# Rounded two-pass products, paired inner products and moved copies in a two-block transformer kernel

## The reference

```python
gdn_qkv = jax.nn.silu(causal_dwconv(gdn_qkv, gdn_conv_w))
g_q = l2_normalize(g_q) * (GDN_HEAD_DIM ** -0.5); g_k = l2_normalize(g_k)
t_inv = lax.linalg.triangular_solve(eye + m, eye, left_side=True, lower=True)   # 64x64 per chunk and head
def step(state, xs):
    v_new = u_c - w_c @ state
    o = q_c @ state + qk_c @ v_new          # qk_c @ v_new: the inner product
    state = state * gl + k_c.T @ v_new
```

```python
q_b = _rotary(q_d, DIFF_ROT); k_b = _rotary(k_d, DIFF_ROT)      # 16 of 64 channels turned
merged = sigmoid(...) * (y_a @ w_branch_a) + sigmoid(...) * (y_b @ w_branch_b)
x = _layer_norm(DEEPNORM_ALPHA * x + merged @ w_out, ...)
```

## Time and profile before

| | |
|---|---|
| median of 3 runs | 1514.75 us (1513.74 to 1515.01) |
| profiled execution | 1514.83 us, span 1513.0 us |
| TensorE products busy | 1496.9 us (99%), 11622 records |
| VectorE, ScalarE, GpSimd busy | 947.8, 811.1, 250.5 us |
| DMA | 266.26 MB, mean 176 GB/s |
| chain that ended last | TensorE 94%, VectorE 4%, ScalarE 1% |

### The profile page before, as it was taken

One profiled execution on the slowest core, in us unless ns is written; L12 is line 12 of the kernel. 1 busy time (PEld: TensorE's weight loads), 2 busy tenths in 40 slices (PEclk: granted clock), 3 DMA queues, 4 the chain that ended last, 5 costly groups with the idle time before them and its releaser, 6 DMA issues.

```text
span 1513.0 us, 27372 instructions
## 1 busy us (share of the span) xinstructions
PE 1496.9 (99%) x11622; PEld 1384.2 (91%) x11622; DVE 947.8 (63%) x1379; ACT 811.1 (54%) x1249; POOL 250.5 (17%) x140
## 2 busy tenths in 40 slices
PE   9999999999999999999999999999999999999998
PEld 8998898889998889998898989998789999899997
DVE  6655466776555475654558685655477766767756
ACT  6554376545544364554574554544365675555762
POOL 0000252113000260000432040000430004500041
PEclk9999999999999999999999999999999999999999
DMA  9655464236555456555543155555455344553341
GB/s 384 226 195 194 159 210 143 79 110 229 190 196 195 167 204 222 195 195 190 195 173 113 59 190 200 194 195 195 167 209 195 112 140 152 208 188 136 131 149 56
DMA packets 39720, 266.26 MB, mean 176 GB/s; under 512 B 4460, under 2 KB 4716, under 8 KB 9392
## 3 DMA queue, kind: packets, MB, share of 16 engines
q1 hardware_dynamic: 38304, 260.13, 48.8%
q0 software_dynamic: 720, 3.35, 0.6%
q10 hardware_dynamic: 576, 1.05, 0.2%
HBM read 263.46 MB, written 1.05 MB: 175 GB/s over the span
## 4 chain that ended last, share of the span: by engine, by line
PE 94%; DVE 4%; ACT 1%; DMA 0%; issue 0%; SPq 0%; DVEq 0%
PE PS L487 17%; PE PS L488 17%; PE PS L489 16%; PE PS L501 6%; PE PS L503 6%; PE PS L502 6%; PE PS L559 4%; PE PS L562 4%; PE PS L560 4%; PE PS L470 1%; PE PS L471 1%; PE PS L472 1%; PE PS L614 1%; PE PS L1942 1%; DVE rawL L319 1%; PE PS L1351 1%
## 5 line engine op out<-in xcount | busy, mean ns | idle before, releaser
L487 PE MATMUL PS<-xTH,WH 128*128 128x256 f32 x2256 | 641.2, 284 | 0.0
L488 PE MATMUL PS<-xTL,WH 128*128 128x256 f32 x2256 | 628.7, 279 | 0.0
L489 PE MATMUL PS<-xTH,rawL 128*128 128x256 f32 x2256 | 626.6, 278 | 0.0
L316 ACT ACTIVATE WH<-raw 128x1024 fp32r<-128x1024 f32 (+2 forms) x476 | 484.6, 1048 | 131.1 <-PE PS L562 101.3
L319 DVE TENSOR_TENSOR rawL<-raw,WH 128x1024 fp32r<-128x1024 f32 (+1 forms) x395 | 481.4, 1245 | 102.5 <-ACT WH L316 102.2
L487 PEld LDWEIGHTS PS<-xTH,WH 128*128 128x128 f32 x2256 | 423.6, 188 | 9.2 <-issue 6.7
L488 PEld LDWEIGHTS PS<-xTL,WH 128*128 128x128 f32 x2256 | 423.7, 188 | 3.4 <-issue 2.9
L489 PEld LDWEIGHTS PS<-xTH,rawL 128*128 128x128 f32 x2256 | 424.9, 188 | 0.0
L319 POOL TENSOR_TENSOR rawL<-raw,WH 128x1024 fp32r<-128x1024 f32 (+1 forms) x81 | 196.1, 2443 | 1049.8 <-ACT WH L316 1049.8
L316 ACT ACTIVATE sg<-PS 128x256 f32<-128x256 f32 x79 | 30.3, 384 | 177.6 <-PE PS L489 177.6
L319 DVE TENSOR_TENSOR hh<-PS,sg 128x256 f32<-128x256 f32 x79 | 33.5, 424 | 144.7 <-ACT sg L316 144.7
(11 more groups left out here) (366 smaller groups left out, 2004.7 us busy)
## 6 DMA issues: line engine op xcount, KB each, us to landing
raw<-in_weights SPq DMA_DIRECT2D x233, 1024.0 KB, 4.8
gb<-in_lngb SPq DMA_DIRECT2D x16, 512.0 KB, 5.1
raw<-in_weights SPq DMA_DIRECT2D x2, 1056.0 KB, 4.9
gb<-in_ln SPq DMA_DIRECT2D x4, 512.0 KB, 4.5
cst<-in_consts POOLq DMA_DIRECT2D x1, 1378.5 KB, 10.4
x0T<-in_xT ACTq DMA_DIRECT2D x4, 256.0 KB, 5.5
raw<-in_weights SPq DMA_DIRECT2D x4, 256.0 KB, 5.1
xt<-in_x POOLq DMA_DIRECT2D x1, 1024.0 KB, 17.3
```

The source lines that it names most:

```text
L316: return Q.put("act", waits, lambda e: e.activation(out, in_, func, **kw))
L487: e.matmul(out, c, xTH[:, k, :], start=k == 0, stop=False)
L488: e.matmul(out, c, xTL[:, k, :], start=False, stop=False)
L489: ins = e.matmul(out, u.L(i, 128 * k, 128), xTH[:, k, :], start=False, stop=k == KD - 1)
```

## The change

- `squares`: ScalarE squares into `sqH` (rounded), VectorE forms `sqL = sq - sqH`, and TensorE makes two rounded passes with a rounded matrix of ones. The same for `rotary` with `permR`: copy, low part `rl`, two passes; the cosine product now reads PSUM.
- The copy of T goes from VectorE to ScalarE.
- The inner products of chunks 0 and 1, and of 2 and 3, go together, in turn on two quadrants.
- In the tail of the second block no split goes to GpSimd.

```diff
@@ mix
+                                h = act(sqH[m][:, :].rearrange("p (j s) -> p j s", j=2), dst, ACT.Square, [a, sq_free[m]])
+                                conv_ready[nm, i] = (m, y, h)
...
         def squares(nm, i):
-            m, a = conv_ready[nm, i]
+            m, y, h = conv_ready[nm, i]
             b, free = bank("B")
-            p = pe([a, free], lambda e: e.matmul(PS[:, b, :], ones, sq[m][:, :], start=True, stop=True))
+            lo = tt(sqL[m][:, :], sq[m][:, :], sqH[m][:, :].bitcast(F32), ALU.subtract, [y, h])
+            def fn(e):
+                e.matmul(PS[:, b, :], onesR[:, :], sqH[m][:, :], start=True, stop=False)
+                return e.matmul(PS[:, b, :], onesR[:, :], sqL[m][:, :], start=False, stop=True)
+            p = pe([ones_rounded(), h, lo, free], fn)
...
-            T_ready = copy(T[:, :, :], PS[:, b, :].rearrange("p (i s) -> p i s", i=8), [p])
+            T_ready = act(T[:, :, :], PS[:, b, :].rearrange("p (i s) -> p i s", i=8), ACT.Copy, [p])
...
+        def inner(c):
+            bs = {x: bank("B") for x in (c - 1, c)}
+            def fn(e):
+                for h in range(4):
+                    for x, (b, _) in bs.items():
+                        R = slice(64 * (x % 2), 64 * (x % 2) + 64)
+                        ins = e.matmul(PS[other(x), b, 128 * h:128 * h + 128], Eu[R, 4 * (x // 2) + h, :], news[x][0][:, h, :], start=True, stop=True)
+                return ins
+            p = pe([news[c - 1][1], news[c][1], qt[c // 2], [free for _, free in bs.values()]], fn)
...
+            if a_ == 1:
+                inner(c)
+                out_sum(c - 1)
+                out_sum(c)
...
@@ second, rotary
             a = act(w[:, :, :], v2(b), ACT.Copy, [p, rw_free[i]])
-            release(b, a)
-            c = tt(pr[:, :, :], w[:, :, :], two(C("dcos")), ALU.mult, [a, pr_free[0]])
+            lo = tt(wl[:, :, :], v2(b), w[:, :, :].bitcast(F32), ALU.subtract, [a])
+            c = tt(pr[:, :, :], v2(b), two(C("dcos")), ALU.mult, [p, pr_free[0]])
+            release(b, a, lo, c)
...
-                p2 = pe([a, free], lambda e: e.matmul(PS[:, b2, :], C("perm"), w[:, :, :].rearrange("p j s -> p (j s)"), start=True, stop=True))
+                    e.matmul(PS[:, b2, :], permR[:, :], w[:, :, :].rearrange("p j s -> p (j s)"), start=True, stop=False)
+                    return e.matmul(PS[:, b2, :], permR[:, :], wl[:, :, :].rearrange("p j s -> p (j s)"), start=False, stop=True)
+                p2 = pe([perm_ready, a, lo, free], fn)
...
@@ second, tail
-        st["share"] = True
+        pump(st["split"] + 1)
```

More of the change, by code:

```diff
@@ L852, in ffn, with ones_rounded @@
         yield
+    ones_ready = []
+    def ones_rounded():
+        if not ones_ready:
+            ones_ready.append(act(onesR[:, :], ones, ACT.Copy, [par_ready]))
+        return ones_ready[0]
     PLE_AT = 55 * 1024
@@ L975, in mix @@
         sq = [put_at("sqa", [128, 512], 12), put_at("sqb", [128, 512], 14)]
+        sqH = [put_at("sqHa", [128, 512], 63, F32R), put_at("sqHb", [128, 512], 65, F32R)]
+        sqL = [put_at("sqLa", [128, 512], 12, F32R), put_at("sqLb", [128, 512], 14, F32R)]
         rs = [put_at("rsa", [128, 512], 16), put_at("rsb", [128, 512], 61)]
@@ L1582, in gate @@
             gate_ready[t] = split(gH[:, :, T_], gL[:, :, T_], yg[t][:, :, :], [y])
+        def inner(c):
[7 more added lines that the diff above has]
+            p = pe([news[c - 1][1], news[c][1], qt[c // 2], [free for _, free in bs.values()]], fn)
+            for x, (b, _) in bs.items():
+                outs_[x] = (b, p, qss[x])
+        news, qss = {0: (u_[0:64, 0, :, :], uts[0])}, {0: None}
         for c in range(4):
@@ L1586, in mix @@
             R, Ro = slice(64 * a_, 64 * a_ + 64), other(c)
-            qs = None
             if c == 0:
-                new, newt = u_[R, 0, :, :], uts[0]
                 next(fill)()
@@ L1598, in mix @@
                 p = pe([state, wts[c], qts[c], free], fn)
[L1599 to L1604, removed]
+                newt = tt(vn[R, :, :], u_[R, t, :, :], PS[R, b, :].rearrange("p (h s) -> p h s", h=4), ALU.subtract, [p, uts[t]])
+                news[c] = vn[R, :, :], newt
+                if c == 2:
+                    normed(0)
+                qss[c] = act(os_[Ro, :, :], PS[Ro, b, :].rearrange("p (h s) -> p h s", h=4), ACT.Copy, [p, on_ready.get(c - 2), qts_all])
+                release(b, newt, qss[c])
                 if c < 3:
@@ L1607, in mix @@
                              ALU.mult, [state, glt], "pool")
-                out_sum(c - 1)
                 next(fill)()
@@ L1611, in mix @@
                 b, free = bank("B")
+                new, newt = news[c]
                 def fn(e, b=b, t=t, R=R, new=new):
@@ L1625, in mix @@
                 sb_soft(0)
[L1626 to L1637, removed]
+            if c == 2:
+                normed(1)
+            if a_ == 1:
+                inner(c)
+                out_sum(c - 1)
+                out_sum(c)
+                if c == 1:
+                    rms(0)
+                    rms(1)
+                else:
+                    gate(0)
             next(fill)()
+        rms(2)
+        go(1)
+        rms(3)
         normed(2)
-        out_sum(3)
-        go(2)
-        rms(3)
         go(2)
         normed(3)
-        go(1)
+        go(2)
         pump(len(chunks))
@@ L1675, in second @@
         va = put_at("va", [128, 2, 512], 32)
-        rw = [put_at("rwa", [128, 2, S], 36), put_at("rwb", [128, 2, S], 38)]
+        rw = [put_at("rwa", [128, 2, S], 36, F32R), put_at("rwb", [128, 2, S], 38, F32R)]
+        rl = [put_at("rla", [128, 2, S], 70, F32R), put_at("rlb", [128, 2, S], 72, F32R)]
+        rs_, permR = put_at("rsum", [128, 2, S], 74), put_at("permR", [128, 128], 76, F32R)
         pr = put_at("pr", [128, 2, S], 40)
@@ L1742, in second @@
         xw = [xT_ready[0], xT_ready[1], par_ready]
+        perm_ready = act(permR[:, :], C("perm"), ACT.Copy, [xw])
         lp = PAR(l, "lam", 0, 256).rearrange("p (a b d) -> p a b d", a=2, b=2)
@@ L1785, in rotary, with fn @@
             rw_n[0] += 1
-            w = rw[i]
+            w, wl = rw[i], rl[i]
             a = act(w[:, :, :], v2(b), ACT.Copy, [p, rw_free[i]])
-            release(b, a)
-            c = tt(pr[:, :, :], w[:, :, :], two(C("dcos")), ALU.mult, [a, pr_free[0]])
+            lo = tt(wl[:, :, :], v2(b), w[:, :, :].bitcast(F32), ALU.subtract, [a])
+            c = tt(pr[:, :, :], v2(b), two(C("dcos")), ALU.mult, [p, pr_free[0]])
+            release(b, a, lo, c)
             def later():
                 b2, free = bank("B")
-                p2 = pe([a, free], lambda e: e.matmul(PS[:, b2, :], C("perm"), w[:, :, :].rearrange("p j s -> p (j s)"), start=True, stop=True))
-                s = tt(w[:, :, :], v2(b2), two(C("dsin")), ALU.mult, [p2, c])
+                def fn(e):
+                    e.matmul(PS[:, b2, :], permR[:, :], w[:, :, :].rearrange("p j s -> p (j s)"), start=True, stop=False)
+                    return e.matmul(PS[:, b2, :], permR[:, :], wl[:, :, :].rearrange("p j s -> p (j s)"), start=False, stop=True)
+                p2 = pe([perm_ready, a, lo, free], fn)
+                s = tt(rs_[:, :, :], v2(b2), two(C("dsin")), ALU.mult, [p2, c])
                 release(b2, s)
-                y = tt(dst, pr[:, :, :], w[:, :, :], ALU.add, [s, c])
+                y = tt(dst, pr[:, :, :], rs_[:, :, :], ALU.add, [s, c])
                 rw_free[i] = y
```

8 lines of the change are left out of this document (3 added, 5 removed).

## The result

The changed kernel takes 1538.61 us (median of 4 runs, 1538.1 to 1540.6) against 1514.88 us of the kernel before beside it: ratio 1.016, 95% interval 1.0143 to 1.0178, 23.7 us slower. Its profiled execution spans 1536.6 us (before: 1513.0).

A forecast was written before the change was run, and what follows sets the result against it. TensorE, busy 1496.9 of 1513.0 us, was taken to bound the kernel. Gains of 15.9 against costs of 31.4, mostly 28.0 of `squares` waits, gave net +15.5: 1514.8 to 1530.3 us; own range 1525 to 1537, 8-in-10 range 1520 to 1545.

The forecast's parts named there:

- likeliest case: The forecast itself: whole kernel net +15.5 us, to 1530.3 us; chance 0.62.
- rival 1: TensorE's clock falls in the new `squares` waits, slowing products behind them: up to 16 us, half taken, 1538; chance 0.22.
- passes on TensorE, `squares` and rotary: 16 constant-matrix products in two rounded passes instead of one fp32 product: gain 0.40 us each, 6.4 in all.
- k0, k1, q0 waits: At `squares`, TensorE waits for `sqL` behind VectorE's six convolution steps: 2.3, 4.3 and 4.3 us a layer.
- q1 waits: At `squares` of q1, `sqL` stands behind three normalisations and a weight split: wait 3.1 us a layer.
- Gram products: Their 0.5 us of waiting goes, since q1's wait lets VectorE catch up.
- inner products: Pairs of chunks alternating on two quadrants cost what one chunk did: gain 4.0 us, bounds 0 to 4.0.
- `scL` and tail of the chunks: Moved VectorE sums and one more split ahead of the short convolution's low part: +0.3 us, at most 2 x 1.22.
- rotary, whole edit: Second block: 3.2 us gained on passes, against waits of 0.7 at the permutation and 2.4 for a bank.
- tail splits: Second block: twice seven splits move from GpSimd to VectorE; the `mt` wait goes, -0.7 us, bounds -0.7 and +1.4.
- The round trip: At `squares` of k1 and q0, TensorE to ScalarE to VectorE and back: an unshortened wait of 4.3 us each.
- third rival: At `squares`, `sqL` is there when TensorE comes, in all eight places: the 28.0 us go, 1502.3; chance 0.06.

The follow-up runs named there:

- wait_filled: Changed kernel with small fp32 products queued on TensorE ahead of the `squares` products of k0, k1, q0 and q1; 1533.8 us, ratio 1.013.
- sq_undone: Changed kernel with the `squares` products back in one fp32 product, all else as changed; 1508.58 us, ratio 0.9963.
- t_alone: Kernel before with only the copy of T moved to ScalarE; 1510.78 us, ratio 0.9971.
- rot_sq_undone: Changed kernel with both `squares` and rotary products back in fp32; 1508.55 us, ratio 0.9958.
- share_back: Changed kernel with all rounded products back in fp32 and every second tail split on GpSimd again; 1509.49 us, ratio 0.9967.
- sq_alone: Kernel before with the `squares` edit alone; 1547.43 us, ratio 1.0214.
- lo_early: Changed kernel with the `sqL` subtraction queued right behind the squares, ahead of the next pair's six convolution steps on VectorE; 1523.63 us, ratio 1.0063.
- split_held: Changed kernel with all rounded products in fp32 and no weight split queued during the last two quarters ahead of the mix's output product; 1505.97 us, ratio 0.9945.
- early_no_share: As `lo_early`, but weight splits stay on VectorE while k and q are projected; 1512.33 us, ratio 0.9981.
- lo_pool: Changed kernel with `sqL` of k0, k1, q0 on GpSimd, no shared splits there, k1's product a quarter later, q1 in fp32; 1512.41 us, ratio 0.9982.
- after: The changed kernel itself, with all edits, against the kernel before; 1538.61 us, ratio 1.016.

## Why the prediction was right, and where it was off

The sign, the place and the mechanism of the waits were right: slower, at `squares`, behind the convolution steps. The time of the likeliest case (1530.3) was 8.3 us short of the measured; the range held because rival 1, the falling clock, is what happened. The failed step is that choice: the forecast took the 4.3 us waits as too short for the clock to fall, at 0.62 against 0.22. Its own sign of being wrong, the granted clock leaving full speed after the waits, came true; that the range still holds the time is due to its having been widened for rival 1.

| term | predicted, us | shown |
|---|---|---|
| passes on TensorE, `squares` and rotary | -6.4 | not measured alone; a rounded pass is 0.23, the first behind a wait 0.31 |
| k0, k1, q0 waits | +21.8 | 21.2 in the list, 22.1 from start to start |
| q1 waits | +6.2 | 0: the slow stretch filled them (in `wait_filled` 2.9 and 2.8 are back) |
| Gram products | -0.5 | -0.5: gone from the list, though q1 did not wait |
| low clock | 0 (rival 1: +8) | about 10.2, of which 4.8 on the path (`wait_filled`) |
| `squares`, whole edit | +24.8 | +29.5 to +30.0 (`sq_undone`) |
| T | -4.3 | -4.3 (`t_alone`) |
| inner products | -4.0 | 3.9 by the distance of the traces |
| `scL` and tail of the chunks | +0.3 | `scL` +1.7, `ez` +1.3 |
| rotary, whole edit | -0.1 | 0 within some 0.8 (`rot_sq_undone`) |
| tail splits | -0.7 | -0.8 in waits (`share_back`); 13 splits left GpSimd (77 to 64), not 14 |

- **The round trip.** The estimate of 4.3 us a wait, made from TensorE's arrival, ScalarE's scaled copies, the six steps and the subtraction, came out at 4.15 and 4.16. VectorE sat idle for 4.92 us before those steps, and the subtraction's inputs were there from 225.70 on, 4 us before the steps began: only the order in the queue held it.
- **The clock.** Five of six such waits were followed by the low level. After 4.2 us it came every time, here and in `sq_alone` (eight of eight). After 1.8 to 2.3 us it came in seven of ten cases: one of two here, two of two in `sq_alone`, four of six in `lo_early`. After waits of up to 1.4 us it never came. So the argument that a 4.3 us wait is too short between stretches of dense work failed clearly: in most cases half of that was enough. Rival 1 gave +8 by halving a bound of 16, and found the hidden part in q1. Its sum (1538) met the measured time partly by luck: on the path the clock cost 5 us in place of 8, and the other 3 us or so came from the chunks.
- **The chunks.** The inner products gained what two quadrants promised:

```profile
311.07 0.32 PE L1607 MATMUL PS<-u,Eu 64*64 64x128 f32 x1
311.08 0.32 PE L1607 MATMUL PS<-vn,Eu 64*64 64x128 f32 x1
...
312.09 0.38 PE L487 MATMUL PS<-xTH,WH 128*128 128x256 f32 x1
```

  Eight products in 1.02 us, two starting 0.01 apart, where four took 1.01. But the term of +0.3, bounded by 2 x 1.22, took a value near the wrong end of its bounds: it was 1.7 at `scL`. Its reason was wrong too: not one split more stands ahead of `scL`, but one sum (`split_held`). The wait of 0.3 for `ez` a layer was not named at all; its distance grows by 0.6 there, 1.3 in both. What moved ahead of `ez` on VectorE was not tried apart.
- **Rotary.** The waits are those predicted, 0.6 and 0.3 at the permutation (0.7 predicted) and 1.3 and 1.0 at the value product (2.4). The list puts the 1.3 down to `kT`, whose last piece ahead of the product ends at 1175.68; `pr` ends at 1175.57 and the product starts at 1175.72, the same 0.15 behind it as at `squares`.
- **The third rival** (`sqL` there in time) was taken as one thing, the order. `lo_early` shows it to be two: once the order was changed, GpSimd's splits met VectorE's and gave half of it back.

Open: why the low clock follows seven of the ten waits of 1.8 to 2.3 us and not the others, and the last 3 us or so of `early_no_share` and `lo_pool` over fp32 `squares`, of which the lists explain the waits at k1, q0 and the Gram products but not what each queue would need.

## What to carry to other kernels

A product that gets cheaper on the bound engine but now needs one more step from another engine is priced by that step's place in the other queue, not by its length: here 0.4 us of gain a product stood against waits of 2 to 4 us. A wait on TensorE should be priced with its aftermath, here 1.4 to 2.6 us lost to half pace behind a wait: always behind 4.2 us, in most cases already behind 2 us, and not on the path where something later would have waited anyway. Before a step is moved between or along VectorE and GpSimd, look at what the other one runs there: when a VectorE operation takes both inputs from SBUF and a GpSimd operation reads SBUF, the later one stands still.

## What the runs showed of the hardware

- The granted clock fell to half (0.50) after TensorE had been idle for 4.2 us, eight times of eight, and after 1.8 to 2.3 us, seven times of ten (`after`, `sq_alone`, `lo_early`); the stretches held 10 to 23 weight products. It never fell after waits of up to 1.4 us. It need not be low at once: behind k1's wait of the first layer the two passes ran at full pace (0.47 and 0.39 us), and the products were slow from 233.78 to 236.97. Small fp32 products in the idle time prevented it altogether.
- VectorE and GpSimd, both with all inputs in SBUF, exclude each other in whole instructions: 2.85 us for 0.69 and 3.43 for 1.22 on VectorE, 2.37 for 1.09 on GpSimd. The six convolution steps, which read one operand from PSUM, kept their 2.43 us beside a GpSimd split (k0: from 219.71, GpSimd's from 220.01 for 2.39).
